# A streaming encoder step on one core: sample tile projected first, no barrier ahead of the attention, buffers of both stages placed anew

## The reference, cut to what matters

```python
h = rms_norm(x, g_norm_mix) * (1 + sc_a) + sh_a             # modulation from silu(c) @ w_ada
proj = h @ w_in                                             # q latent 256 | kv latent 128 | rotary key 32 | u 512 | v 512
q = rms_norm(rms_norm(q_lat) @ w_uq)                        # 8 heads of 96, the last 32 rotated
k, v = rms_norm(ckv) @ w_ukv                                # the same for new and cached latents
att = softmax(mask(q @ k.T)) @ v                            # block-causal over chunks of 64
v_rows = layer_norm(gelu(g_v))
gm = gelu(g_u) * (w_spatial @ v_rows + b)                   # chunks of 128 rows
x = x + gt_a * (concat(rms_norm(att), rms_norm(gm)) @ w_out)
x = x + gt_m * hier_moe(rms_norm(x) * (1 + sc_m) + sh_m)    # top-1 group, top-2 experts of 8
```

## Time and profile before

| | us |
|---|---|
| median of three runs (1190.32 to 1192.72) | 1191.31 |
| the profiled execution's own time | 1195.41 |
| its span in the profile | 1193.7 |
| TensorE busy | 1086.5 (91%) |
| VectorE busy | 640.8 (54%) |
| GpSimd, ScalarE busy | 318.1, 271.8 |

### The profile page before, as it was taken

One profiled execution on the slowest core, in us unless ns is written; L12 is line 12 of the kernel. 1 busy time (PEld: TensorE's weight loads), 2 busy tenths in 40 slices (PEclk: granted clock), 3 DMA queues, 4 the chain that ended last, 5 costly groups with the idle time before them and its releaser, 6 DMA issues.

```text
span 1193.7 us, 14240 instructions
## 1 busy us (share of the span) xinstructions
PE 1086.5 (91%) x4836; PEld 706.3 (59%) x4836; DVE 640.8 (54%) x1274; ACT 271.8 (23%) x606; POOL 318.1 (27%) x351
## 2 busy tenths in 40 slices
PE   4599999999478889998999999989999999999993
PEld 1245555554246545666667666777777777777771
DVE  2445555555525356556667576826665445445452
ACT  1132322222142121223232321121111211112110
POOL 1122222222240111011011000014345445454543
PEclk9899999999858799999999999779999999999997
DMA  9873334341170132234032124657989898998940
GB/s 318 328 289 143 145 142 151 144 151 69 44 191 5 62 106 104 83 114 150 28 124 89 45 103 195 242 219 276 362 304 349 333 367 337 347 349 332 357 178 16
DMA packets 78038, 229.55 MB, mean 192 GB/s; under 512 B 29828, under 2 KB 33559, under 8 KB 62231
## 3 DMA queue, kind: packets, MB, share of 16 engines
q1 hardware_dynamic: 50544, 198.63, 44.6%
q0 software_dynamic: 24048, 26.81, 6.7%
q10 hardware_dynamic: 3382, 3.32, 0.8%
HBM read 201.23 MB, written 88.25 MB: 243 GB/s over the span
## 4 chain that ended last, share of the span: by engine, by line
PE 77%; DVE 11%; issue 3%; ACT 3%; DMA 3%; POOL 2%; ACTq 1%; DVEq 0%; POOLq 0%; SPq 0%
PE bank L968 15%; PE bank L1310 10%; PE bank L1312 10%; PE bank L1327 9%; PE bank L923 9%; PE bank L1131 8%; PE bank L1077 5%; PE bank L1102 4%; PE bank L1049 2%; PE bank L951 2%; PE bank L935 1%; PE bank L978 1%; POOL st L776 1%; DMA grope<-in_g_knorm 1%; DVE probT L2068 1%
## 5 line engine op out<-in xcount | busy, mean ns | idle before, releaser
L968 PE MATMUL bank<-W_in,hT 128*128 128x512 f32 (+3 forms) x432 | 180.4, 571 | 3.3 <-ACTq L1448 3.3
L775 POOL TENSOR_SCALAR st<-st 128x1 f32<-128x1 f32 (+6 forms) x76 | 17.5, 230 | 603.4 <-DVEq L1668 603.4
L968 PEld LDWEIGHTS bank<-W_in,hT 128*128 128x128 f32 (+1 forms) x432 | 79.3, 186 | 94.0 <-issue 88.5
L1131 PE MATMUL bank<-W_out,mT 128*128 128x512 f32 (+1 forms) x256 | 124.1, 614 | 0.0
L1327 PE MATMUL bank<-WD,hidT 128*128 128x512 f32 x264 | 120.7, 600 | 2.9 <-DVE hidT L2276 2.9
L1310 PE MATMUL bank<-WG,xT 128*128 128x256 f32 x528 | 121.9, 385 | 1.0 <-DVE xT L2260 1.0
L1312 PE MATMUL bank<-WU,xT 128*128 128x256 f32 x528 | 119.3, 379 | 0.0
L1312 PEld LDWEIGHTS bank<-WU,xT 128*128 128x128 f32 x528 | 100.3, 190 | 13.6
L1310 PEld LDWEIGHTS bank<-WG,xT 128*128 128x128 f32 x528 | 99.4, 193 | 14.0 <-issue 1.4
L2068 DVE COPY probT<-bank 128x512 f32<-128x512 f32 (+3 forms) x104 | 57.0, 548 | 68.3 <-PE bank L923 60.1
L1077 PE MATMUL bank<-kT,qT 104*128 104x512 f32 (+4 forms) x224 | 91.3, 524 | 0.7 <-ACTq L1542 0.7
(11 more groups left out here) (320 smaller groups left out, 1480.0 us busy)
## 6 DMA issues: line engine op xcount, KB each, us to landing
WG<-in_w_gate_e SPq DMA_DIRECT2D x33, 1024.0 KB, 7.0
WU<-in_w_up_e SPq DMA_DIRECT2D x33, 1024.0 KB, 9.2
WD<-in_w_down_e SPq DMA_DIRECT2D x33, 1024.0 KB, 12.9
ada_w<-in_w_ada SPq DMA_DIRECT2D x24, 1024.0 KB, 7.4
residual_scratch<-x_att SPq DMA_DIRECT2D x32, 512.0 KB, 4.4
kbuf<-k_scratch SPq DMA_DIRECT2D x12, 384.0 KB, 5.3
xbuf<-in_x_prompt SPq DMA_DIRECT2D x8, 512.0 KB, 3.8
W_in<-in_w_in SPq DMA_DIRECT2D x2, 2048.0 KB, 18.6
```

The source lines that it names most:

```text
L968: ins = mm(ps[:R, 0:n], hT[:, t % 2, k, :R], W_in[:, k, c0:c0 + n], start=(k == 0), stop=(k == KD - 1))
L1131: ins = mm(bank[:R, :], (mT_last if s == LAST else mT)[:, k, :R], W_out[:, k, half * 512:(half + 1) * 512], start=(k == 0), stop=(k == KD ...
```

## The change

The projection loop now runs over places `i` of `seq` (sample first, then prompt tiles 0 to 7), and double buffers go by `i % 2`. The barrier is gone. In the last tile (`END`, prompt tile 7) the key/value projection moves ahead of the gate values, and its banks are set by hand. The last `mix` moves behind the preparation of the first attention tile on TensorE and, on VectorE, behind the first two row maxima. Constants of the attention are made in the last tile. SyncE's first attention loads wait for the sample's own stores and for the last gate-value projection; stores of the last tile come after them. Broadcast rows move from heads 2 and 3 to heads 6 and 7. `prob` and `probT` change places with `tmp2` and `bc_next`; `gate_m` and `gate_w` move too, and ScalarE waits for the last `h2` before it fills `gate_m`.

```diff
+    b1 = Banks(psum[0:7], f1, e1, order1, {("kv0", END): 4, ("kv1", END): 5, ("gv", END): 0, ("q0", END): 2, ("q1", END): 3, ("mix", END): 6})
...
-        if s == 0 and h in (2, 3):
-            work += [("vectors", h - 2, 0)]
+        if s == 0 and h in (6, 7):
+            work += [("vectors", h - 6, 0)]
...
+    def filled(eng, tag):
+
+        b, use, _ = b1.at[tag]
+        eng.wait_ge(f1[b], use + 1)
+
+    def stored_keys(eng, kts):
+
+        for par in range(2):
+            n = [key_order.index(kt) // 2 + 1 for kt in kts if key_order.index(kt) % 2 == par]
+            if n:
+                eng.wait_ge(s_out1[f"k{par}"], 16 * max(n))
+                eng.wait_ge(s_out1[f"v{par}"], 16 * max(n))
...
@@ SyncE @@
             if t == SAMPLE:
-                sp.wait_ge(s_vr, t + 1)
+                sp.wait_ge(s_vr, i + 1)
                 sp.dma_start(v_s[0, 0], vrows[:R]).then_inc(s_out1["vs"], 16)
+            if i < LAST:
+                store_q(i)
...
-        sp.sem_inc(s_end1, 1)
-        sp.wait_ge(s_end1, 4)
...
+        stored_keys(sp, key_tiles[SAMPLE])
+        sp.wait_ge(s_out1["q"], 16)
+        filled(sp, ("gv", END))
         new_keys(0)
+        store_kv(sp, END)
+        store_q(LAST)
+        stored_keys(sp, key_order)
+        sp.wait_ge(s_out1["q"], 16 * len(seq))
+        new_keys(1)
+        store_gm(LAST)
+        for k, m in (("lat0", 2 * (NT // 2 + 1)), ("lat1", 2 * (NT // 2)), ("gm", NT + 1), ("vs", 1)):
+            sp.wait_ge(s_out1[k], 16 * m)
...
@@ GpSimd @@
-        g.sem_inc(s_end1, 1)
-        g.wait_ge(s_end1, 4)
+        filled(g, ("q1", END))
+        g.wait_ge(s_rs, n_roots)
         do(g.memset(first_rows[QK:KM, :], 0.0))
...
+        rstd(st[:P, 41:42], st[:P, 41:42])
+        g.wait_ge(s_rs, n_roots)
         do(g.tensor_copy(kT[QK:KM, 1:H, :], bcast(kT[QK:KM, 0:1, :], [NT, H - 1, SEQ])))
...
@@ TensorE @@
+            if i == LAST:
+                pe.wait_ge(s_latT, i + 1)
+                kv(END)
             proj(t, "gv", LAT + GW, GW)
...
-        kv(NT)
-        mix(NT)
-        pe.wait_ge(s_end1, 4)
-
+
+        def freed(bank):
+
+            pe.wait_ge(e1[bank], b1.total[bank])
...
+        freed(4)
+        freed(5)
         prep(0)
+        mix(LAST)
+        freed(0)
+        freed(1)
         S(0, 0)
+        freed(2)
+        freed(3)
         S(0, 1)
...
@@ ScalarE @@
+            act.wait_ge(s_h2, LAST + 1)
             for half in range(2):
                 do(A(gate_m[:, v, half * 512:(half + 1) * 512], psum[3 + 2 * v + half][:], ACT.Copy))
...
@@ VectorE @@
+            if i == LAST:
+                attend_constants()
+                kv(END)
...
+            if i == 1:
+                dve.wait_ge(s_out1["vs"], 16)
...
-        kv(NT)
-        mix(NT)
-        signal(s_end1)
-        dve.wait_ge(s_end1, 4)
...
         def rows_of_vectors(s):
+            if s:
+                stored_keys(dve, key_order)
+                dve.wait_ge(s_out1["q"], 16 * len(seq))
+                dve.wait_ge(s_out1["gm"], 16 * len(seq))
+                for par in range(2):
+                    dve.wait_ge(s_out1[f"lat{par}"], 32 * len(range(par, len(seq), 2)))
...
         row_max(0, 0)
         row_max(0, 1)
+        mix(LAST)
```

More of the change, by code:

```diff
@@ L83, with __init__ @@
 class Banks:
-    def __init__(self, tiles, filled, freed, order):
+    def __init__(self, tiles, filled, freed, order, places={}):
         self.tiles, self.filled, self.freed = tiles, filled, freed
@@ L90, in __init__ @@
         for n, (tag, readers) in enumerate(order):
-            b = n % len(tiles)
+            b = places.get(tag, n % len(tiles))
             assert tag not in self.at, tag
@@ L400, in build_in, with loop_ada, kvs @@
     act_step, dve_step, pool_step = (Signal(sem(f"{n}_step")) for n in ("act", "dve", "pool"))
-    def loop_ada(t):
-        return [KD + 2 * t, KD + 2 * t + 1]
+    def loop_ada(i):
+        return [KD + 2 * i, KD + 2 * i + 1]
     ADA_AT = {NT // 2: 1, NT: 2}
-    def kvs(t):
-        return ([9 + NC_ - 1] if t == 0 else [t - 1])
+    seq = [SAMPLE] + list(range(NT))
+    LAST = len(seq) - 1
+    END = seq[LAST]
+    place_of = {t: i for i, t in enumerate(seq)}
+    def kvs(i):
+        return ([9 + NC_ - 1] if i == 0 else [seq[i - 1]])
     early_keys = list(range(9, 9 + NC_ - 1))
-    key_order = early_keys + [kt for t in range(NT + 1) for kt in kvs(t)] + [NT]
+    key_order = early_keys + [kt for i in range(NT + 1) for kt in kvs(i)] + [END]
     kv_use = lambda kt: [(("kv0", kt), 3), (("kv1", kt), 3)]
@@ L461, in build_in @@
     e2 = [sem(f"ring_freed{i}") for i in range(2)]
-    seq = [SAMPLE] + list(range(NT))
     key_tiles = {SAMPLE: [9 + c for c in range(NC_)] + [SAMPLE]} | {t: [t] for t in range(NT)}
@@ new lines, in _ @@
+        for i, t in enumerate(seq):
+            R = ROWS[t]
+            sp.wait_ge(s_lat, i + 1)
+            sp.dma_start(ckv_rows[t], lat[:R, i % 2, QL:QL + KVL]).then_inc(s_out1[f"lat{i % 2}"], 16)
+            sp.dma_start(kr_rows[t], lat[:R, i % 2, QL + KVL:]).then_inc(s_out1[f"lat{i % 2}"], 16)
+            if i + 2 <= LAST:
+                sp.wait_ge(s_xn, i + 1)
+                x_load(i + 2)
+            if i < LAST:
+                for j in loop_ada(i):
+                    ada(j)
+            if i == 0:
+                sp.dma_start(W_out[:], w["w_out"][0].rearrange("(k p) n -> p k n", p=P)).then_inc(s_wout, 16)
+            for kt in kvs(i):
+                store_kv(sp, kt)
+            if i:
+                store_gm(i - 1)
@@ L1470, in _ @@
         hT_half(0)
-        for t in range(NT + 1):
+        for i, t in enumerate(seq):
             R = ROWS[t]
             ps = b1.read(act, ("lat", t))
-            if t >= 2:
-                act.wait_ge(s_out1[f"lat{t % 2}"], 32 * (t // 2))
-                act.wait_ge(s_kh, key_order.index(t - 2) + 1)
-            done(A(lat[:R, t % 2], ps[:R, 0:LAT], ACT.Copy), b1.free(("lat", t)))
+            if i >= 2:
+                act.wait_ge(s_out1[f"lat{i % 2}"], 32 * (i // 2))
+                act.wait_ge(s_kh, key_order.index(seq[i - 2]) + 1)
+            done(A(lat[:R, i % 2], ps[:R, 0:LAT], ACT.Copy), b1.free(("lat", t)))
@@ L1494, in _ @@
-            done(A(u_sb[:R, t % 2], ps[:R, :], ACT.Gelu_apprx_tanh), b1.free(("u", t)))
+            if i >= 2:
+                act.wait_ge(s_gm, i - 1)
+            done(A(u_sb[:R, i % 2], ps[:R, :], ACT.Gelu_apprx_tanh), b1.free(("u", t)))
             act.wait_ge(b1.free(("u", t)), b1.at[("u", t)][2] + 1)
             act.sem_inc(s_u, 1)
-            if t < NT:
-                hT_half(t + 1)
+            if i < LAST:
+                hT_half(i + 1)
+            else:
+                kv(END)
@@ L1851, in _ @@
             signal(s_qh)
[L1853 to L1854 removed]
+            if i:
+                k = i - 1
                 if k == 0:
```

294 lines of the change are left out of this document (142 added, 152 removed).

## The result

| | median, us | lowest to highest | runs | ratio to the kernel before |
|---|---|---|---|---|
| before | 1191.77 | 1187.50 to 1193.38 | 10 | |
| changed | 1185.73 | 1179.22 to 1188.21 | 10 | 0.9943 [0.9924, 0.9963] |

Measured again twice, on other chips, it gave 0.9925 [0.9909, 0.9942] and 0.9935 [0.9911, 0.9960]: 7.8 and 7.3 us by the medians, 8.9 and 7.7 by the ratios. So the change makes the kernel faster by 6 to 9 us, in place of the 16.2 forecast, and the time of 1185.7 lies outside the range of 1168 to 1184.

What follows compares the result with a forecast made beforehand. TensorE was taken to set the time nearly everywhere, with the barrier between the stages a hole in it. Terms -0.4 - 20.6 + 0.8 + 3.0 + 1.0 = -16.2 us took 1191.3 to 1175 us, range 1168 to 1184.

Steps and rivals of the forecast that it cites:

- Start of the attention: Boundary of projection and attention: without the barrier, first scores start at 323.7 instead of 344.34; -20.6 us, bounds -21.3 and -18.5.
- the first tile's -0.4: Start of the projection: the 64-row sample tile goes first, with shorter hT copies and half the x load; -0.4 us.
- VectorE late at the first row maxima: First attention head: GpSimd's mask instructions hold up VectorE's queue ahead of the first row maximum; +0.8 us, bounds 0 and +4.
- Last gMLP tile between row maxima and probability copies: First heads, on VectorE: the tile takes 3.7 us against 1.4 of slack, delaying TensorE; +3.0 us, bounds 2 and 4.5.
- rival (b): VectorE becomes the bound at the seam through mask instructions, the 6.16 copy and gMLP; -9.3 us, 1182 us, chance 0.13.
- Broadcast jobs moved: Heads 6 and 7 instead of 2 and 3: both jobs may run at half clock; +1.0 us, bounds -1 and +3.
- Clock: Sample tile's heads: TensorE keeps the same half clock as before; 0 us, bounds -5.5 and +5.
- rival (a): TensorE's clock stays at full from preparation on; -21.7 us, 1169.6 us, chance 0.13 together with everything beyond -19.5.
- (c): Rival: TensorE's low-use stretches join into one long half-clock stretch; +27 on the forecast, +10.8 us, 1202 us, chance 0.04.

Runs made afterwards that it cites:

- fence: Changed kernel with GpSimd's long mask copy held back until VectorE has scaled the last gMLP tile; 1177.70 us, 0.9862, and again 1178.01 us, 0.9873.
- spread: Changed kernel with VectorE's last gMLP tile in three parts, at heads 1, 2 and 3, and GpSimd's mask copy ahead of the root; 1176.23 us, 0.9865.
- after_again: The changed kernel run again unaltered, as base of another group and for a second profile; 1183.31 us, 0.9925 of the kernel before.
- vec67: Kernel before with only the two broadcast-row jobs moved from heads 2 and 3 to heads 6 and 7; 1197.90 us, 1.0030.
- fill: fence plus 32 useless 128-column matmuls on TensorE, in the sample tile's preparation and behind its second and third scores; 1167.91 us, 0.9802.
- vec23: fence with the whole broadcast jobs back at heads 2 and 3 of the sample tile; 1174.45 us, 0.9865, and again 1172.11 us, 0.9847.
- before_fill: Kernel before with eighty useless matmuls over its barrier and the same ones as fill behind it; 1189.17 us, 0.9971.
- barrier: Changed kernel with the barrier put back and the last mix ahead of it, all else as changed; 1194.36 us, 1.0020.
- after_side: The changed kernel run again unaltered, as base of a further group, with a third profile; 1184.71 us, 0.9935 of the kernel before.

## Why the prediction was wrong

Direction and place were right: a chance of 0.93 stood on faster. The time was 10.7 us too low. The steps:

- **Start of the attention** (-20.6; first scores at 323.7). Measured 322.63. Gate values at 302.37 (predicted 302.4), `kbuf` at 312.74 (312.8), mix at 320.19 (321.7), taking 2.50 (2.0). Right within 1.5 us; of the first tile's -0.4 nothing shows, as the last gate-value projection starts at 302.37 where 302.4 was worked out without it, but 0.4 us is less than executions differ by at this place.
- **VectorE late at the first row maxima** (+0.8). It was not: it waited 1.84 us for the scores at 324.92. It did meet the mask instruction, in `rot` (0.80 at 320.25, against 0.42 at 289.34 in the tile before), with no effect. The meeting was milder than the one that the term was taken from: `rot` ends at 321.05, 1.48 us before the mask instruction does (319.66 + 2.87), and the three rotation instructions behind it, with two SBUF inputs each and wholly under that instruction, took their usual 0.62 (for two) and 0.42. All three profiles of the changed kernel show this. The earlier trace rows do not show a block for the whole length either, though the prediction read them so: the sum loses 0.81 us beside an instruction of 3.88, and that 3.88 is itself drawn out. GpSimd's same mask instruction takes 2.87 at 319.66 above, and 3.88 where it starts 0.14 us into another VectorE instruction of two SBUF inputs (435.16 to 436.44, line 1914, in the kernel before). Row maxima and probability copies beside the long copy (in `fence`) kept their times, as the prediction said by the rule in the Trainium skill, "SBUF — State Buffer", "Who interferes with whom". The same rule has some `tensor_scalar` instructions contend too, and the rows at 331.46 and 331.49 agree on the whole block; its other half, that the one that issues first wins, is not borne out by the records here, where VectorE starts 0.03 us first and loses; 0.03 us may be too little to go by.
- **Last gMLP tile between row maxima and probability copies** (+3.0, bounds 2 and 4.5). This is the term that failed. The wait is 8.29. The tile's own work was right (in `fence` it ends at 333.41, which leaves 2.31 of wait); what was left out is that GpSimd's 6.16 us copy follows the root in GpSimd's queue and so starts with the scaling. The prediction listed the copy as "ready some 15 us before head 6 wants it", which is true (the first scores that read it start at 363.68, 26 us after its end) and beside the point, and put the block only into rival (b) at "about 3". Taking the block away gave 6.7 us in the medians (7.4 in the ratios) of one group. With the 3.0 for the tile's own work the term is about +10, not +3. Only the block's 7 of it are measured: `spread`, which takes the rest of the wait away too, is no faster than `fence`, and 7.1 us below `after_again`.
- **Broadcast jobs moved** (+1.0, bounds -1 and +3). Mis-sized: +3.6 measured alone, 3 to 4 most likely in the changed kernel. The argument looked at the clock. Another account was not tested by itself: at heads 2 and 3 the six copies fill VectorE's idle time in heads of 4.1 us, at 6 and 7 VectorE is late for the short heads of the next tile. The waits show 1.3 us of that (`vec67`); the rest of the cost stays open.
- **Clock** (0). As predicted, the half clock held to 361 us, and neither rival (a) nor (c) came. The reason given, the gap at the first heads, is not borne out: in the first profile the clock had fallen ahead of that gap (0.50 from 322 to 324), and in `spread`, where nothing longer than 0.72 us is left of it, it was 0.50 all the same. So this zero was right in part by luck. `fill` shows that the state of rival (a) can be had, with 32 idle matmuls in preparation and first heads.

The sum with the two terms corrected: -16.2 + 7.0 (block) + 2.6 (3.6 for 1.0) = -6.6, against -6.0, -7.8 and -7.3 measured. `fence`, with the block gone, came to 1177.7, 15.8 below its base. `vec23` has both undone: without block and move the forecast's own sum is -17.2, and it came to -16.1 and -18.2 by the ratios (-19.3 and -19.9 by the medians). The profiles agree in the main. From the first to the fourth preparation the kernel before takes 106.2 us, the changed kernel 117.2, 117.8 and 115.0, `fence` 112.6 twice, `vec23` 107.8 and 107.9. Of the 9 to 12 us lost there, 2 to 5 go with the block and close to 5 with the broadcast jobs, so these weigh more here than `vec67` alone says; under 2 stay unexplained. Rival (b) named the mechanism and a time of 1182, at a chance of 0.13; its share for the block, "about 3", was half of what it is.

Still open: whether the block costs more than the 6.0 us for which VectorE stands (6.7 to 7.4 measured, inside the noise of these runs), why the clock falls where it does, and how much the broadcast move costs the changed kernel, where 3 to 4 us rests on medians more than on intervals.

## What to carry to other kernels

When a transfer or a barrier is taken away, write out the queue of every engine across the seam, GpSimd's too, and ask for each long instruction what it starts together with, not only when its result is needed. A long GpSimd copy right behind the small root that releases a VectorE instruction met it in every profile here; one wait or a cut into pieces gives the time back. When work is moved, name the stretch that it leaves as well as the one that it goes to: here the jobs hid part of the loss in the one and made that of the other. And where TensorE waits briefly in a stretch at half clock, matmuls of no use placed in it can be worth as much as the change itself (7 to 9 us here, on top of `fence`); placed in the open they cost what they take (5.0 of 7.1 in `before_fill`).

## What the runs showed of the hardware

- A VectorE `tensor_scalar` from SBUF to SBUF (0.48 us) beside a GpSimd copy stood for all of it: 6.47 with a 6.15 us copy, 1.35 with one of 1.1. In both VectorE's record starts 0.03 us before GpSimd's. VectorE instructions that read PSUM were not touched (0.42 and 0.68 beside the 6.16 us copy).
- The other way round, GpSimd's `memset` of the key mask took 1.38 us where it started 0.27 us behind VectorE's `W_out` scaling (322.58 and 322.31), and 0.95 in the kernel before and in `barrier`, where VectorE was idle.
- A VectorE instruction with two SBUF inputs did not stand for the whole of a GpSimd one: `rot` took 0.80 instead of 0.42 beside one of 2.87 us, the three behind it their usual times, and the sum at line 1917 2.76 instead of 1.946 beside one of 3.88. That one was itself held by the VectorE instruction ahead of the sum; it took 2.86 where VectorE did little (both in the kernel before):

```profile
331.62 2.86 POOL L808 TENSOR_SCALAR qT<-first_rows,ident 8x1024 f32<-8x1024 f32 x1
...
435.16 1.28 DVE L1914 SCALAR_TENSOR_TENSOR tmp<-x_att,st,A 64x1024 f32<-64x1024 f32 x1 [1.15 <-POOL st L776]
```

- 32 matmuls of 128 columns took the granted clock of a 21 us stretch from 0.50 to 1.00, and the kernel from 0.9862 and 0.9873 to 0.9802 of the time before. With TensorE recorded as busy for 16.97 of 17 us the clock still stood at 0.50 (`spread`).
- The changed kernel's runs spread over 9 us (1179.22 to 1188.21) on one core; its first two profiles differ by 4.6 us in span, and agree within 0.3 us at the fourth preparation; the third, `after_side`, is 2 us ahead of them there (427.95).
